# Prompt attention of a hybrid decoder step: both KV groups at once, pipelined by one item

## The chip, the core and the metric

The kernel runs on one core of a Trainium2 chip. The metric is the device time of one execution in microseconds (us); less is better. Engines are named as in the profile: PE (TensorE, matmuls; PEld is its weight load), DVE (VectorE), ACT (ScalarE), POOL (GpSimd) and SP (SyncE, which issues DMAs). Each engine works through its own queue in order, and engines wait for one another by semaphores.

## What is computed

One step of one decoder layer: a half feed-forward block, a mixer, a second half feed-forward block and a final norm, for a prompt of 512 tokens and for 8 sampled sequences of one token with 2048 past tokens. The mixer runs a short convolution beside an attention with three branches: compressed keys, selected blocks of keys, and a window. There are 8 heads in 2 KV groups of 4, each of 64 columns. For the prompt, as 512 tokens have no more blocks than the selection takes and no more tokens than the window, selected and window branches are both plain causal attention, each on its own keys and values. Cut to what matters:

```python
def nsa_core(q, t, kc, vc, kb, vb, kw, vw, kw_pos, gates):
    s = jnp.einsum('btghd,bngd->btghn', q, kc).astype(jnp.float32) * scale
    p_cmp = jax.nn.softmax(jnp.where(m, s, NEG), axis=-1) * m
    o_cmp = jnp.einsum('btghn,bngd->btghd', p_cmp.astype(vc.dtype), vc)
    ...
    s = jnp.einsum('btghd,btgnkd->btghnk', q, kg).astype(jnp.float32) * scale
    ...
    o_sel = jnp.einsum('btghnk,btgnkd->btghd', p.astype(vg.dtype), vg)
    s = jnp.einsum('btghd,bkgd->btghk', q, kw).astype(jnp.float32) * scale
    ...
    o_win = jnp.einsum('btghk,bkgd->btghd', p.astype(vw.dtype), vw)
    return gates[..., 0:1] * o_cmp + gates[..., 1:2] * o_sel + gates[..., 2:3] * o_win
```

## The kernel before

All data stay in SBUF with features or tokens on the 128 partitions; weights are streamed from HBM. A weight unit is split by ACT into a high part (`hi`, L623) and by POOL into the remainder (`lo`, L534), and `unit` (L1454) multiplies them on PE. This holds for the feed-forward blocks, the mixer's input projection, the merge (units U_M3 and up) and the output projection. Between the input projection and the merge lies the attention; for the sampled tokens first their keys are turned and scored, then the prompt's compressed keys are built, then comes the stage that is changed.

The stage is a loop over j, four head pairs: head j of group 0 on partitions 0 to 63 of `Q[:, j]`, head j of group 1 on partitions 64 to 127. For each j there are six blocks b = 0 to 5: compressed, selected and window branch of group 0, and the same of group 1. To multiply with one group alone, DVE copies that group's half of Q into `qz`, whose other half is zero (`queries`, L1156), so that every score is a full 128-row matmul. Blocks go through these steps:

- scores (PE, L1610): four matmuls of 128 to 512 key columns, query tile q seeing keys up to its own tile, into PSUM banks 0 to 3; compressed scores (31 keys) into bank 7;
- `stage1` (DVE, L1201): adds the causal mask and takes the row maximum in one instruction (L1220) from PSUM to `sm`, then scales the maximum (L1225);
- `exps` (ACT, L824): exponentials in place, with row sums;
- `stage2` (DVE, L1227): reciprocal of the sum times the branch's gate, then four multiplications (L1250) that scale the probabilities;
- `turns` (PE, L1629): ten 128x128 transposes (L1354) into banks 4 and 5 by turns, emptied by ACT (`empty`, L820);
- `values` (PE, L1647): four matmuls of 64 output partitions into bank 6, on the half that belongs to the group; all six blocks of a j add up there, and the result is split by ACT (`oth`) and DVE (`otl`).

PE's order is written out by hand in `attend` (L1677): for each block its turns, then the scores of the block two further on, then its values. Twice in a j a sampled sequence is put in between (`sampled`, L1662): 21 matmuls over 2 MB of rows in `GB`, which POOL gathers by an indirect DMA (L531) into one of two buffers once the pass that used it is done, and over `wt`, loaded by SP. The result is added up by DVE (L1255, L1258). The last j is written apart: it holds the first merge unit U_M3 between blocks 4 and 5, whose weights ACT splits right behind the last sampled pass.

```python
            def attend(j, last):
                for b in range(6):
                    ...
                    turns(b, j)
                    if b < 4:
                        scores(b + 2, j)
                    ...
                    if b == 0:
                        sampled(j, 0)
                    values(b, j)
                    if b == 3:
                        sampled(j, 1)
```

## Time and profile before

| what | value |
|---|---|
| median of 3 runs | 1541.0 us (1540.9 to 1541.74) |
| profiled execution, first to last instruction (span) | 1539.9 us |
| profiled execution's own time | not listed apart; 1.1 us lie between its span and the median |
| PE, PEld busy | 1482.3 us (96%), 1377.8 us (89%) |
| DVE, ACT, POOL busy | 642.2 (42%), 538.7 (35%), 504.8 us (33%) |
| mean granted PE clock | 0.986 |

Busy time is the time in which an engine had an instruction under way; matmuls are pipelined, so a start-to-start distance tells more than a duration. Durations in the texts are in us unless marked ns. A granted clock of 1.00 is 2.4 GHz, 0.50 is 1.2 GHz. In a row, `out<-in` names the tiles, L is the line in the kernel, and what stands in brackets is idle time before the instruction and what ended it.

### The profile page before, as it was taken

Reading aid. Unit: us, or ns where it says so; the run is one execution under the profiler, and the core shown is the slowest. Engines: PE = TensorE matmul, PEld = TensorE weight load, DVE = VectorE, ACT = ScalarE, POOL = GpSimd, SP = SyncE. Lnnn points to the kernel's source line nnn. Section 1 sums busy time; section 2 is a strip of 40 time slices with the busy share of each in tenths; the row PEclk is TensorE's granted clock in tenths of the full one; section 3 lists DMA queues with packets and bytes.
Section 4 is the critical chain, followed back from the end, with each engine's and each line's share of the span. In section 5 each row is a group of like instructions: output and inputs, shape, how many; then the busy total and the mean of one; then the engine's idle time right before and its main releaser. Section 6 shows DMA issues by size and latency. Waiting matters only on the chain.

```text
span 1539.9 us, 27584 instructions
## 1 busy us (share of the span) xinstructions
PE 1482.3 (96%) x11500; PEld 1377.8 (89%) x11500; DVE 642.2 (42%) x996; ACT 538.7 (35%) x808; POOL 504.8 (33%) x222
## 2 busy tenths in 40 slices
PE   4899999999999999999899999999899999999998
PEld 4899999999999999994376666999899999999997
DVE  5777533220234652953045553211584332023353
ACT  5566644311223222213344443432334432122221
POOL 3100644443444333410100001444444445344440
PEclk9999999999999999999979999999999999999999
DMA  6731132331323523227833331333232233222221
GB/s 192 253 131 55 55 110 82 119 100 55 105 87 103 198 83 83 84 110 276 301 124 132 134 136 60 97 89 102 84 109 83 82 126 95 81 82 82 95 69 55
DMA packets 125457, 173.08 MB, mean 112 GB/s; under 512 B 11658, under 2 KB 118850, under 8 KB 122236
## 3 DMA queue, kind: packets, MB, share of 16 engines
q1 hardware_dynamic: 121372, 121.98, 25.3%
q0 software_dynamic: 3456, 50.33, 8.1%
q8 instruction: 40, 0.66, 0.2%
q14 instruction: 13, 0.11, 0.0%
q10 hardware_dynamic: 576, 0.00, 0.0%
HBM read 168.55 MB, written 7.95 MB: 115 GB/s over the span
## 4 chain that ended last, share of the span: by engine, by line
PE 92%; DVE 3%; DMA 2%; ACT 1%; issue 1%; SPq 0%; ACTq 0%; DVEq 0%
PE bank L1468 69%; PE bank L1410 5%; PE bank L1354 5%; PE bank L1658 2%; PE bank L1626 2%; PE bank L1671 2%; PE bank L1570 2%; DMA GB<-cache_sel_kv,idx 1%; PE bank L1598 1%; DMA XC<-cache_cmp_kv,idx 1%; PE bank L1618 1%; PE bank L1654 1%; PE bank L1673 0%; DVE XT1l L922 0%; DVE tmp L990 0%
## 5 line engine op out<-in xcount | busy, mean ns | idle before, releaser
L540 POOL TENSOR_TENSOR wlo<-raw,whi 128x1024 fp32r<-128x1024 f32 (+3 forms) x183 | 460.6, 2518 | 633.5 <-ACT whi L644 633.1
L644 ACT ACTIVATE whi<-raw 128x1024 fp32r<-128x1024 f32 (+3 forms) x183 | 196.5, 1075 | 655.4 <-PE bank L1468 649.2
L1468 PE MATMUL bank<-xh,whi 128*128 128x260 f32 (+1 forms) x2032 | 410.0, 283 | 2.9 <-issue 1.1
L1468 PE MATMUL bank<-xh,wlo 128*128 128x260 f32 (+1 forms) x2032 | 409.4, 283 | 0.0
L1468 PE MATMUL bank<-xl,whi 128*128 128x260 f32 (+1 forms) x2032 | 408.7, 283 | 0.0
L1468 PEld LDWEIGHTS bank<-xh,whi 128*128 128x128 f32 (+1 forms) x2032 | 312.6, 188 | 5.1 <-issue 2.2
L1468 PEld LDWEIGHTS bank<-xh,wlo 128*128 128x128 f32 (+1 forms) x2032 | 312.4, 188 | 0.3
L1468 PEld LDWEIGHTS bank<-xl,whi 128*128 128x128 f32 (+1 forms) x2032 | 311.6, 188 | 0.3
L1010 DVE TENSOR_TENSOR tmp<-bank,rr 128x520 f32<-128x520 f32 x88 | 61.6, 700 | 276.6 <-PE bank L1468 275.9
L1468 PE MATMUL bank<-hl,whi 128*128 128x260 f32 x704 | 141.9, 283 | 0.0
L1468 PE MATMUL bank<-hh,wlo 128*128 128x260 f32 x704 | 141.6, 282 | 0.0
L1468 PE MATMUL bank<-hh,whi 128*128 128x260 f32 x704 | 141.3, 282 | 0.0
L1468 PEld LDWEIGHTS bank<-hh,whi 128*128 128x128 f32 x704 | 108.5, 188 | 0.0
L1468 PEld LDWEIGHTS bank<-hh,wlo 128*128 128x128 f32 x704 | 108.4, 188 | 0.0
L1468 PEld LDWEIGHTS bank<-hl,whi 128*128 128x128 f32 x704 | 108.3, 188 | 0.0
L1017 DVE TENSOR_TENSOR hl<-tmp,hh 128x520 f32 x44 | 90.9, 2066 | 40.2 <-ACT hh L735 40.2
L1024 DVE SCALAR_TENSOR_TENSOR xT<-bank,xT 128x520 f32<-128x520 f32 x32 | 22.4, 700 | 161.1 <-PE bank L1468 161.1
L531 POOL DMA_INDIRECT GB<-cache_sel_kv,idx x16 | 15.1, 942 | 223.1 <-PE bank L1674 129.4
L1354 PE MATMUL bank<-ident,XC 128*128 128x128 f32 x256 | 43.1, 298 | 11.9 <-DMA XC<-cache_cmp_kv,idx 10.7
L961 DVE TENSOR_TENSOR tmp<-tmp,tmp 128x520 f32<-128x520 f32 x21 | 53.5, 2547 | 0.7
L922 DVE TENSOR_TENSOR XT0l<-bank,XT0h 64x512 fp32r<-64x512 f32 x64 | 44.2, 690 | 16.5 <-ACT XT0h L675 15.9
L922 DVE TENSOR_TENSOR XT1l<-bank,XT1h 64x512 fp32r<-64x512 f32 x64 | 44.1, 690 | 15.4 <-ACT XT1h L675 14.1
(273 smaller groups left out, 1881.9 us busy)
## 6 DMA issues: line engine op xcount, KB each, us to landing
raw<-ffn_w_gate SPq DMA_DIRECT2D x22, 1024.0 KB, 5.3
raw<-ffn_w_up SPq DMA_DIRECT2D x22, 1024.0 KB, 5.3
raw<-w_mix_in SPq DMA_DIRECT2D x17, 1024.0 KB, 5.1
raw<-ffn_w_down SPq DMA_DIRECT2D x8, 1536.0 KB, 6.5
raw<-ffn_w_down SPq DMA_DIRECT2D x8, 1280.0 KB, 5.8
wt<-win_kv_sample SPq DMA_DIRECT2D x16, 512.0 KB, 3.9
raw<-w_mix_out SPq DMA_DIRECT2D x4, 1024.0 KB, 4.9
win_kv_sample<-state_win_kv SPq DMA_DIRECT2D x1, 4088.0 KB
```

What stands on the lines that cost most here:

```text
L540: pool.tensor_tensor(tile(wlo, w, k, u), raw_tile(u), tile(whi, w, k, u).bitcast(F32), ALU.subtract)\
L644: act.activation(dst, src, ACT.Copy).then_inc(hi_done, 1)
L922: ins = tt(dst, src, hi_.bitcast(F32), ALU.subtract)
L961: ins = tt(ssq[:, :], ssq[:, :], tmp[6][:, :], ALU.add)
L1010: tt(two(dst[:, :]), acc(g), two(rr[:, :]), ALU.mult).then_inc(acc_free, 1)
L1017: tt(hl[:, c, :].rearrange("p o t -> p (o t)"), tmp[1 + j][:, :], hh[:, c, :].rearrange("p o t -> p (o t)").bitcast(F32), ALU.subtract).th ...
L1354: return pe.transpose(dst, src, ident[0:n, 0:n])
L1410: ins = pe.matmul(hid, w[:, kk, j, :], x[kk][b % 2][:, s, r:r + NCMP, :].rearrange("p c g -> p (c g)"), start=(s + r + n == 0), stop=(s == ...
L1468: ins = pe.matmul(acc(g)[0:m, h, :], w[:, u % WS, c, 0:m], x[:, c, h * HT:(h + 1) * HT], start=(c == 0 and n == 0), stop=(c == k - 1 and n ...
L1570: pe.matmul(bank[0:64, q % 5, :], qps[q // 5][:, :], kt[q % 2][:, :], start=False, stop=False, skip_group_check=True).then_inc(kt_used, 1)
L1626: pe.matmul(bank[:, q, 0:(q + 1) * P], qz[:, g, q * P:(q + 1) * P], k[:, 0:(q + 1) * P], start=True, stop=True)\
L1658: ins = pe.matmul(out[:, k * P:SEQ], rows[:, k, c:c + HD], ptp[:, k, k * P:SEQ], start=False, stop=(b % 3 == 2 and k == 0))
```

## The change

The loop now runs over eight items n; item n is head pair j = n // 2 and the selected (n even) or window branch (n odd), for both groups at once. `qz` and its copies are gone: scores take 64 rows of `Q` and of the keys, group 0 on rows 0 to 63 and group 1 on rows 64 to 127, into two banks, with the groups alternating; the four banks hold two query tiles at a time, so the later four of eight scores wait until DVE has read the earlier ones. Values alternate between the groups' two halves of the output partitions, 128 columns at a time. The compressed branch is done once a j for both groups, with the keys of both side by side. Transposes go into chunks of four, four and two tiles, whose evictions alternate between ACT and DVE. The scaling of the probabilities moves from DVE to POOL, which has the gathers for the sampled pass in the same queue. The order is one of a pipeline: the scores of n + 1 come ahead of the turns of n. All loops of the stage are written out. The core of the diff:

```diff
+        ITEMS = 2 * HPG
+
+        def chunk_no(n, g, c):
+
+
+            first = n // 2 * 13 + n % 2 * 7
+            return first + (3 if g == 2 else c if g == 0 else (4 if n % 2 == 0 else 3) + c)
+
+        def chunk_size(c):
+            return (4, 4, 2)[c]
 
         def load_pages(eng, first):
...
-                    else:
-                        pool.wait_ge(sv_done, b - 1)
-                    gather(GB[b % 2], 1, b, gb_loaded[b % 2])
+            for b in range(DB):
+                if b == 0:
+                    pool.wait_ge(lo_done, U_M3)
+                elif b == 1:
+                    pool.wait_ge(grp_done, group(U_M3 - 2) + 1)
+                else:
+                    pool.wait_ge(tp_done, TB + 5 * (b - 1))
+                gather(GB[b % 2], 1, b, gb_loaded[b % 2])
+            for b in range(2):
+                pool.wait_ge(tp_done, TB + 5 * (DB - 1 + b))
+                gather(GB[b % 2], 1, b, gb_loaded[b % 2])
+            for n in range(ITEMS):
+                for g in range(KVH):
+                    pool.wait_ge(fct_ready, 2 * n + g + 1)
+                    for q in range(QT):
+                        v = sm[n % 2][g][:, q * (q + 1) // 2 * P:(q + 1) * (q + 2) // 2 * P]
+                        pool.tensor_scalar(v, v, fct[:, n % 2, q, g:g + 1], None, ALU.mult).then_inc(big_p, 1)
+                if n + 2 < DB:
+                    pool.wait_ge(sv_done, n + 1)
+                    gather(GB[n % 2], 1, n + 2, gb_loaded[n % 2])
...
+            exps(0, 0)
+            for n in range(ITEMS):
+                j = n // 2
+                exps(n, 1)
+                if n % 2 == 0:
+                    cmp_exps(j)
+                    if j:
+                        out_hi(j - 1)
+                empty(n, 0)
+                if n + 1 < ITEMS:
+                    exps(n + 1, 0)
+                else:
+                    act.wait_ge(sv_done, DB)
+                    hi(U_M3)
+                if n % 2 == 0:
+                    empty_cmp(j)
+                empty(n, 1)
+            hi(U_M3 + 1)
+            out_hi(HPG - 1)
 
             for u in range(2, 4):
...
+            def big_max(n, qs):
+
+                if qs[0] == 0 and n >= 2:
+                    dve.wait_ge(pt_tp, chunk_no(n - 2, 1, 2) + 1)
+                for q in qs:
+                    for g in range(KVH):
+                        dve.wait_ge(big_s, 8 * n + 2 * q + g + 1)
+                        dve.memset(bump[:, 4 + 2 * q + g:5 + 2 * q + g], 0.0)
+                        dve.tensor_tensor_reduce(sm[n % 2][g][:, q * (q + 1) // 2 * P:(q + 1) * (q + 2) // 2 * P],
+                                                 bank[:, 2 * (q % 2) + g, 0:(q + 1) * P], tri[:, SEQ - (q + 1) * P:SEQ], 1.0, -3e38,
+                                                 ALU.add, ALU.max, nmx[:, n % 2, q, g:g + 1])\
+                            .then_inc(big_rd, 1)
+
+            def big_neg(n):
+
+                dve.wait_ge(big_rd, 8 * n + 8)
+                ts(nmx[:, n % 2, :, :], nmx[:, n % 2, :, :], -SCALE, None, ALU.mult).then_inc(big_nm, 1)
+
+            def factors(n, g):
+
+                dve.wait_ge(big_exp, 8 * n + 4 * g + 4)
+                pp.did(dve.reciprocal(fct[:, n % 2, :, g], lsm[:, n % 2, :, g]))
+                pp.wait()
+                tt(fct[:, n % 2, :, g], fct[:, n % 2, :, g], gates(n // 2, 1 + n % 2)[:, :, g], ALU.mult).then_inc(fct_ready, 1)
...
+            for n in range(ITEMS):
+                j = n // 2
+                if n + 1 < ITEMS:
+                    big_max(n + 1, range(3))
+                    factors(n, 0)
+                    big_max(n + 1, range(3, QT))
+                    big_neg(n + 1)
                 else:
-                    dve.wait_ge(vn_done, 1)
-                    pp.wait()
-                    pp.did(ts(om[:, :], bank[0:64, 7, 3 * P:4 * P], sst[:, 15:16], None, ALU.mult))
-                    pp.wait()
-                    omg = om[:, :].rearrange("p (g d) -> p g d", g=KVH)
-                    pp.did(tt(omg, omg, gmask[:, :].unsqueeze(2).to_broadcast([64, KVH, HD]), ALU.mult))
-                    pp.wait()
-                    tt(o64[:, :], o64[:, :], om[:, :], ALU.add).then_inc(o64_ready, 1)
-                dve.wait_ge(o_hi, j + 1)
-                tt(otl[:, bass.ds(j, 1), 0:SEQ].rearrange("p o t -> p (o t)"), bank[:, 6, :],
-                   oth[:, bass.ds(j, 1), 0:SEQ].rearrange("p o t -> p (o t)").bitcast(F32), ALU.subtract).then_inc(o_lo, 1)
-                if not last:
-                    pp.end(HPG - 1)
-
-            dve.memset(bump[:, 0:1], 0.0).then_inc(sv_rd, 1)
-            stage1(0, 0)
-            stage2(0, 0)
-            stage1(1, 0)
-            with dve.Fori(0, HPG - 1) as j:
-                attend(j, False)
-            attend(HPG - 1, True)
+                    factors(n, 0)
+                factors(n, 1)
+                if n % 2 == 0:
+                    cmp_norm(j)
+                if n % 2 == 0 and j:
+                    out_lo(j - 1)
+                empty(n, 0)
+                sampled(n)
+                if n % 2 == 0:
+                    empty_cmp(j)
+                empty(n, 1)
+                if n % 2 and j + 1 < HPG:
+                    cmp_max(j + 1)
...
+            def scores(n):
+
+
                 for q in range(QT):
-                    pe.wait_ge(big_p, j * 16 + (4 * n + q + 1))
-                    pe.wait_ge(tp_ev, j * 18 + (TBP + t + q - 1))
+                    for g in range(KVH):
+                        r = slice(HD * g, HD * (g + 1))
+                        i = 8 * n + 2 * q + g
+                        if i >= 4:
+                            pe.wait_ge(big_rd, i - 3)
+                        pe.matmul(bank[:, 2 * (q % 2) + g, 0:(q + 1) * P], Q[r, n // 2, q * P:(q + 1) * P],
+                                  kv[r, 4 + n % 2, 0:(q + 1) * P], start=True, stop=True).then_inc(big_s, 1)
...
+            def turns(n, g):
+
+                for c in range(3):
+                    t = chunk_no(n, g, c)
+                    bank_free(t)
+                    for m in range(4 * c, 4 * c + chunk_size(c)):
+                        q = (0, 1, 1, 2, 2, 2, 3, 3, 3, 3)[m]
+                        pe.wait_ge(big_p, 8 * n + 4 * g + q + 1)
+                        ins = turn(bank[:, 4 + t % 2, (m - 4 * c) * P:(m - 4 * c + 1) * P], sm[n % 2][g][:, m * P:(m + 1) * P])
+                    ins.then_inc(pt_tp, 1)
...
+            def values(n):
+
+
+                t = chunk_no(n, 1, 2)
+                for t in (t - 1, t):
+                    pe.wait_ge((pt_act, pt_dve)[t % 2], t // 2 + 1)
+                for q in range(QT):
                     for k in range(q + 1):
+                        for g in range(KVH):
+                            c = (1 + n % 2) * ROW + P + g * HD
+                            ins = pe.matmul(bank[HD * g:HD * (g + 1), 6, q * P:(q + 1) * P], rows[:, k, c:c + HD],
+                                            prob(g, q * (q + 1) // 2 + k), start=False, stop=(n % 2 == 1 and k == QT - 1))
                 ins.then_inc(pv_done, 1)
...
+            for n in range(ITEMS):
+                j = n // 2
+                if n + 1 < ITEMS:
+                    scores(n + 1)
+                else:
+                    sampled(n)
+                turns(n, 0)
+                if n + 1 < ITEMS:
+                    sampled(n)
+                else:
+                    pe.wait_ge(big_rd, 8 * ITEMS)
+                    unit(U_M3, xh, xl)
+                if n % 2 == 0:
+                    turns_cmp(j)
+                turns(n, 1)
+                if n % 2 and j + 1 < HPG:
+                    cmp_scores(j + 1)
+                if n + 1 == ITEMS:
+                    pe.wait_ge(sv_rd, 1 + DB)
+                    pe.matmul(bank[0:64, 7, 3 * P:4 * P], e8[:, :], srows[:, ROW + P:2 * ROW], start=True, stop=True)\
+                        .then_inc(vn_done, 1)
+                if n % 2 == 0:
+                    values_cmp(j)
+                values(n)
```

## Rows read from the trace of the kernel before

**Rows 1.** Busy time by stretches: stretch, length, each engine's busy time, PE clock, DMA.

```profile
797.51:836.26 38.75, 38.11 (x216) 25.16 (x216) 19.04 (x84) 17.08 (x53) 1.88 (x2) 1.00 0.36 136
...
913.79:958.11 44.32, 41.12 (x251) 29.02 (x251) 18.69 (x69) 18.91 (x54) 4.97 (x2) 1.00 0.19 60
```

**Rows 2.** Timeline of PE inside pairs 1 and 2: start us, busy us, line, operands, count.

```profile
855.49 0.62 PE L1354 MATMUL bank<-ident,cm 128*31 128x128 f32 x4
855.95 2.32 PE L1626 MATMUL bank<-kv,qz 128*128 128x128 f32 x8
858.21 1.07 PE L1654 MATMUL bank<-ptc,vcP 31*64 31x512 f32 x2
859.21 3.71 PE L1671 MATMUL bank<-GB,pst 128*64 128x128 f32 x32
...
863.94 1.68 PE L1354 MATMUL bank<-ident,sm 128*128 128x128 f32 x10
865.66 1.07 PE L1618 MATMUL bank<-kcP,qz 128*128 128x31 f32 x8
866.66 2.37 PE L1658 MATMUL bank<-ptp,rows 128*64 128x128 f32 x8
868.96 1.68 PE L1354 MATMUL bank<-ident,sm 128*128 128x128 f32 x10
870.47 2.32 PE L1626 MATMUL bank<-kv,qz 128*128 128x128 f32 x8
```

**Rows 3.** Line L1383 from 51.0 to 51.5 us: count, duration ns min/median/max, starts us.

```profile
L1383 PE MATMUL bank<-SH,w x4: 272/298/323, 51.0 to 51.2; 128*64 128x127 f32 x4
```

**Rows 4.** Busy time by stretches, columns as in rows 1, where the clock changed.

```profile
755.65:759.14 3.49, 0.00 (x1) 0.00 (x1) 0.00 (x0) 0.00 (x0) 0.21 (x1) 1.00 0.98 397
760.37:763.78 3.41, 3.41 (x7) 1.00 (x6) 0.00 (x0) 0.73 (x2) 0.00 (x0) 0.50 1.02 432
774.03:794.50 20.47, 19.98 (x88) 18.14 (x88) 7.50 (x21) 8.18 (x15) 0.00 (x0) 0.50 0.38 137
```

**Rows 5.** Timelines of PE and of DVE at the first scores of all.

```profile
790.88 4.19 PE L1626 MATMUL bank<-kv,qz 128*128 128x128 f32 x8
...
795.21 0.06 DVE L1218 MEMSET bump<- 128x1 f32 x1 [1.79 <-PE bank L1626]
```

**Rows 6.** Timeline of DVE through maxima, factors and scaling of one item.

```profile
839.67 0.29 DVE L1220 CUSTOM_DVE_ANT_0 sm<-bank,tri 128x128 f32<-128x128 f32 x1
...
839.89 0.42 DVE L1220 CUSTOM_DVE_ANT_0 sm<-bank,tri 128x256 f32<-128x256 f32 x1
...
840.24 0.55 DVE L1220 CUSTOM_DVE_ANT_0 sm<-bank,tri 128x384 f32<-128x384 f32 x1
...
840.72 0.69 DVE L1220 CUSTOM_DVE_ANT_0 sm<-bank,tri 128x512 f32<-128x512 f32 x1
...
841.54 0.18 DVE L1244 RECIPROCAL fct<-lsm 128x4 f32<-128x4 f32 x1
...
842.08 1.27 DVE L1250 TENSOR_SCALAR sm<-sm,fct 128x128 f32<-128x128 f32 x4
```

**Rows 7.** POOL by form, 940 to 1000 us: count, busy us, mean ns, idle before, releaser.

```profile
L540 POOL TENSOR_TENSOR wlo<-raw,whi 128x1024 fp32r<-128x1024 f32 x8 | 20.1, 2509 | 57.8 <-ACT whi L644 57.8
L540 POOL TENSOR_TENSOR wlo<-raw,whi 128x512 fp32r<-128x512 f32 x5 | 6.5, 1290 | 8.2 <-ACT whi L644 8.2
```

**Rows 8.** Tile GB: time from the issue of a gather to its landing.

```profile
DMA to landing us min/median/max: 8.5/8.9/12.2
```

**Rows 9.** ACT's and POOL's timelines and the chain in time order, at unit U_M3.

```profile
941.84 1.06 ACT L644 ACTIVATE whi<-raw 128x1024 fp32r<-128x1024 f32 x1 [1.34 <-PE bank L1674]
...
942.98 2.36 POOL L540 TENSOR_TENSOR wlo<-raw,whi 128x1024 fp32r<-128x1024 f32 x1 [39.00 <-ACT whi L644]
...
947.58 5.97 PE bank L1468 x48
```

More of the change, by code:

```diff
@@ L837, in attend @@
-            def attend(j, last):
-                for b in range(1, 5):
-                    exps(b + 1, j)
-                    if last and b == 4:
-                        act.wait_ge(sv_done, DB)
-                        hi(U_M3)
-                    empty(b, j)
-                if last:
-                    hi(U_M3 + 1)
-                empty(5, j)
-                if not last:
-                    exps(0, j, 1)
-                    exps(1, j, 1)
-                act.wait_ge(pv_done, j * 6 + 6)
-                act.activation(oth[:, bass.ds(j, 1), 0:SEQ].rearrange("p o t -> p (o t)"), bank[:, 6, :], ACT.Copy)\
-                    .then_inc(o_hi, 1)
-                if not last:
-                    empty(0, j, 1)
@@ new lines, in _ @@
+            dve.wait_ge(cpo_done, 2)
+            pp.did(dve.memset(cm[0][:], 0.0))
+            pp.wait()
+            cmp_max(0)
+            big_max(0, range(QT))
+            big_neg(0)
+            for n in range(ITEMS):
[5 more added lines that the diff above has]
+                    big_neg(n + 1)
+                else:
+                    factors(n, 0)
[11 more added lines that the diff above has]
+                    cmp_max(j + 1)
@@ L1647, in values @@
-            def values(b, j):
-                g, t = b // 3, [1, 5, 9, 10, 14, 18][b]
-                pe.wait_ge(tp_ev, j * 18 + (TBP + t))
-                out = bank[HD * g:HD * (g + 1), 6, :]
-                if b % 3 == 0:
-                    if g == 0:
-                        pe.wait_ge(o_lo, j + 1)
-                    pe.matmul(out, vcP[:, g * HD:(g + 1) * HD], ptc[:, :], start=True, stop=False).then_inc(pv_done, 1)
-                    return
-                for k in reversed(range(QT)):
-                    c = (b % 3) * ROW + P + g * HD
-                    ins = pe.matmul(out[:, k * P:SEQ], rows[:, k, c:c + HD], ptp[:, k, k * P:SEQ], start=False,
-                                    stop=(b % 3 == 2 and k == 0))
-                ins.then_inc(pv_done, 1)
@@ L1673, in sampled @@
                     pe.matmul(out, pst[:, 16 + t, :], wt[s][:, t, P:2 * P], start=False, stop=False)
-                pe.matmul(out, pst[0:NCMP, 20, :], vcS[:, bass.ds(j * 2 + s, 1), :].rearrange("p o e -> p (o e)"),
-                          start=False, stop=True).then_inc(sv_done, 1)
-            def attend(j, last):
-                for b in range(6):
-                    if last and b == 5:
-                        pe.wait_ge(big_rd, 16 * HPG)
-                        unit(U_M3, xh, xl)
-                    turns(b, j)
-                    if b < 4:
-                        scores(b + 2, j)
-                    elif not last:
-                        if b == 4:
-                            pe.wait_ge(qz_ready, j + 2)
-                        scores(b - 4, j, 1)
-                    if b == 0:
-                        sampled(j, 0)
-                    values(b, j)
-                    if b == 3:
-                        sampled(j, 1)
-                    if b == 4 and last:
-                        pe.wait_ge(sv_rd, 1 + DB)
-                        pe.matmul(bank[0:64, 7, 3 * P:4 * P], e8[:, :], srows[:, ROW + P:2 * ROW], start=True, stop=True)\
-                            .then_inc(vn_done, 1)
-            pe.wait_ge(qz_ready, 1)
+                pe.matmul(out, pst[0:NCMP, 20, :], vcS[:, b, :], start=False, stop=True).then_inc(sv_done, 1)
             pe.wait_ge(cpo_ev, 2)
-            scores(0, 0)
+            cmp_scores(0)
             pe.wait_ge(keys_rd, 1)
-            scores(1, 0)
+            scores(0)
             pe.wait_ge(ps_ready, 1)
```

317 lines of the change are left out of this document (144 added, 173 removed).

## The prediction

> **What bounds the kernel now.** The busy shares of the whole span (table above) say TensorE (PE), 96%, but an average says nothing of this stage. So the first view is the table by stretches, cut at the first probability turn of each head pair j, from which the reader is to see who is idle here. The four pairs run from 797.51 to 958.11 us: 38.75 us for a plain one, 44.32 for the last, which also holds the first merge unit [rows 1]. In the plain one PE is busy for 38.11 us, DVE for 19.04, ACT for 17.08, POOL for 1.88 at full clock: the stage is PE's own work, and only what shortens or idles PE counts. Then the timeline of PE, which prices a pass by the start of one group to the start of the next [rows 2]; one pair holds two of each compressed group and sampled pass and four of the others: compressed turns 0.46, scores of one group and branch 2.26, compressed values 1.00, sampled values 4.73 (859.21 to 863.94), compressed scores 1.00, values 2.30, turns of ten tiles 1.51. One pair is 4 x (1.51 + 2.26 + 2.30) + 2 x (0.46 + 1.00 + 1.00) + 2 x 4.73 = 38.7, as measured.
>
> **Scores, values, compressed branch: what goes.** Values now write two column halves in turn. That halves of columns run together is in the trace: L1383's four 127-column instructions, on two column halves, start within 51.0 to 51.2 us [rows 3]; on one and the same half an instruction of 128 columns takes 0.11 (the sampled pass, 42 in 4.73 [rows 2]), and four starts would spread over 0.33. So values of both groups cost 2.30 an item, not 4.60. For scores on two row halves no row shows a pair. Bounds: 2.26 an item (as columns do) and 4.52 (one after the other); I take 2.26, by the nearest row. The Trainium skill's page "TensorEngine Tiling (Array Packing)", Key Properties, says that different tiles load weights and multiply in parallel; by it the sum is the one taken here, and rows 3 agree for columns only. The compressed branch goes from two of each per pair to one: 2.46 less. PE's own work is then 2.26 + 2 x 1.51 + 4.73 + 2.30 + 1.00 = 13.3 for an odd item and 13.8 (0.46 and 1.00 in place of one 1.00) for an even one, 27.1 a pair.
>
> **What the new order makes PE wait for.** An item issues scores(n+1) and then turns(n, group 0), with sampled(n) behind these, so all waits stand in PE's queue and everything behind waits too. From the start of scores(n+1):
> 1. Four of the eight scores wait for banks that DVE must have read, and DVE works out no factor for item n until it has done the maxima of q = 0 to 2. First scores are seen at about 0.55, an estimate: the second of two instructions starts some 0.1 to 0.15 in, takes 0.27 to 0.32 [rows 3], and DVE began 0.14 after the group that ended at 795.07 [rows 5]. Maxima start 0.22, 0.35 and 0.48 apart [rows 6]; each now has its own memset of 0.06 [rows 5]; two groups: 2 x 1.23 = 2.46. DVE is through at 3.0.
> 2. Reciprocal and gate factor: 0.54 (841.54 to 842.08 [rows 6]). With a hop POOL starts at 3.6.
> 3. POOL multiplies 128 + 256 + 384 + 512 columns, four instructions, in place of DVE. No row shows POOL doing this. Bounds: DVE's four took 1.27 [rows 6]; POOL's own two-input subtraction takes 1.29 for 512 and 2.51 for 1024 columns [rows 7], 2.38 ns a column and 0.07 an instruction, so 3.3. Same operation on one side, same engine on the other: I take the middle, S = 2.3. The Trainium skill's page "GPSIMD Engine Reference", Engine selection, says that one-input work runs at about line rate and two-input work about twice as slow as on VectorE; by it S is near 1.3 and the sum 7 us lower. Rows 7 agree for two inputs, none shows one.
> 4. PE may turn the last four tiles when q = 3 is scaled: 4 x 0.15 = 0.6 and a hop of 0.1. PE leaves turns(n, 0) at 3.6 + 2.3 + 0.7 = 6.6 instead of 2.26 + 1.51 = 3.8. **2.8 us of every item become a wait.**
> Behind it an odd item has sampled 4.73, turns 1.51, compressed scores 1.00, values 2.30: 16.1. Evictions there fit beside the compressed scores. An even item has 0.46 and 1.00 in place of 1.00 and some 0.1 of eviction: 16.6; where DVE, not ACT, evicts the compressed chunk (j even), it first adds up the sampled result, two operations and their waits, 0.5 by estimate: 17.1.
>
> **Covers.** ACT (17.08 of 38.75 [rows 1]) hands half of its evictions to DVE and has over 12 us for each group's exponentials. DVE loses four scalings of 1.27 a pair and gains evictions; factors of group 1, the compressed normalisation, the low half of the output and an eviction must end before sampled(n) does, at 11.3; with POOL done at 3.6 + 2 x 2.3 = 8.2 that is so by over 1 us. POOL's gather for n+2 now stands behind two scalings and the wait for sampled(n), and scaling of n+1 behind it: 0.94 of issue (two in 1.88 [rows 1]) against some 8 us until it is wanted. Its data land 8.9 us after issue, 12.2 at most [rows 8], with over 25 us until sampled(n+2). SP's loads keep their triggers; no DMA is added. If an item shrank below some 10 us, these covers would be gone.
>
> **Start and end.** Scores(0), at half clock, took 4.19 (clock 0.50 up to 794.50 [rows 4, 5]); eight half-row scores move as many columns, but the last wait for DVE, now behind them instead of beside: the loop starts 0.5 later, at 798.0. Item 7 has no scores ahead: sampled 4.73, turns 1.51. Then unit U_M3 needs its weights, and ACT splits these only after its last eviction of that group: eviction and hops 0.7 (estimate), ACT 1.06, POOL 2.36 [rows 9], so PE stands for 4.1; before, this lay beside turns and values. After an idle 3.49 us the clock was at 0.50 for a stretch of 3.41 us [rows 4]; I charge 2.0 for such a fall here (half of that stretch is 1.7). Unit 5.97 [rows 9], turns 1.5, the new key's matmul 0.4 (as the compressed turns), values 2.3 after 0.5 of waiting (estimate), weights of the next unit 0.8 late (ACT and POOL again, from the last ACT eviction, against the rest of the turns and the values): 23.8.
>
> **The sum.** 798.0 + 17.1 (n = 0) + 3 x 16.1 (odd) + 2 x 16.6 (n = 2, 6) + 17.1 (n = 4) + 23.8 = 937.5, against 958.1: 20.6 us less. What follows is unchanged. The span of 1539.9 becomes 1519.3; the profiled execution lies 1.1 under the median of the runs (1541.0), so I add that: **1520**.
>
> **Rivals.**
> *POOL is the bound (slower).* Each us of S costs 7 us (items 0 to 6). At S = 2.3 + 20.6 / 7 = 5.2 the gain is gone; at S = 6 the time is 1520 + 26 = 1546. Against it: the dearest POOL row gives 3.3. For it: the instruction has never run here and takes its factor from memory. 0.06.
> *The clock falls in the gap between scores and sampled values.* PE would have only transposes and waits there for some 3.6 us of each item. The trace has a fall after 3.49 us without work [rows 4] and none in the pairs, where turns follow matmuls closely. One half-clock stretch of 3.41 in each of seven items costs 7 x 1.7 = 12: 1532; twice that long, 1544. 0.17.
> *Halves don't run together* (the change does not do what it says). Columns: 8 x 2.30 = 18 more, 1538. Rows alone: PE then paces DVE, and step 1 ends 0.65 later: 4.5 more, 1525, inside the forecast. 0.05 for columns.
> *The waits are hidden after all,* PE alone sets the pace: items of 13.3 and 13.8 save 7 x 2.8 and a little more, 1500. It would need DVE's maxima to run beside earlier PE work, which the order of its queue forbids. 0.08.
> The forecast itself, S from 1.27 to 3.3 (-7, +7) and rows alone, is 0.64 and covers 1512 to 1532.
>
> **How the numbers follow.** 0.2% (3 us) is what a measurement of this kernel can tell. Faster by more: the forecast (0.64), the hidden waits (0.08), most of the clock's cases (0.12), some of the columns' (0.02): 0.86. Within: 0.05. Slower: POOL (0.05), the long clock falls (0.03), columns with one of these (0.01): 0.09. The range runs to 1507 below (part of the hidden waits) and to 1537 above (the short clock falls), and leaves out POOL as the bound, serial columns and long falls.
>
> **What would show it.** Right: matmuls of values in pairs some ns apart; per item one idle stretch of PE before its turns, put down to POOL's scaling, and 16 to 17 us from one sampled pass to the next; POOL's scaling between 1.3 and 3.3 for four; PE idle about 4 us before U_M3. Wrong: pairs following each other by their full length; granted clock under 1.0 inside the items; idle time of PE put down to DVE's evictions, or to a gather; a scaling over 5 us.

## The result and the profile after

Measured: **1550.0 us** (median of 4 runs, 1549.4 to 1551.3) against 1541.1 for the kernel before on the same chip (4 runs); the ratio is 1.0056 with an interval of 1.0042 to 1.0071. The change made the kernel slower by some 9 us; 1520 was forecast, and 1550 lies above the range of 1507 to 1537.

The page of the profiled execution (1551.3 us), its busy times and its row of granted clock by fortieths of the span:

```profile
PE 1465.8 (95%) x11636; PEld 1383.8 (89%) x11636; DVE 633.5 (41%) x965; ACT 521.0 (34%) x760; POOL 572.9 (37%) x286
PEclk9999999999999999999968888999999999999999
```

The eights stand where prompt attention is. Next the table by stretches (stretch, length, busy time and count of PE, PEld, DVE, ACT, POOL, granted clock, DMA share, GB/s): items 0 to 6 from the first score of item 1 to the sampled pass of item 7; item 1 alone; item 7; and the first and the last of seven stretches, one in each item:

```profile
799.24:944.85 145.61, 120.58 (x874) 94.60 (x875) 63.28 (x272) 51.46 (x159) 68.01 (x65) 0.84 0.30 116
821.37:841.58 20.21, 16.84 (x128) 13.77 (x126) 8.28 (x37) 6.22 (x20) 9.52 (x9) 0.83 0.29 114
944.85:968.46 23.61, 18.51 (x156) 17.03 (x153) 5.08 (x8) 3.75 (x6) 10.95 (x8) 0.86 0.15 45
...
806.61:813.44 6.83, 5.84 (x28) 5.48 (x28) 1.23 (x3) 3.00 (x10) 5.21 (x5) 0.50 0.01 2
...
929.50:936.30 6.80, 5.56 (x23) 4.43 (x24) 3.10 (x7) 2.77 (x9) 6.22 (x6) 0.50 0.01 4
```

Before, a pair (two items) took 38.75 us at full clock with PE idle for 0.6 [rows 1]. Now item 1 alone takes 20.21: PE idles for 3.4 of it, and the clock is 0.83, since in every item some 6.8 us run at its lower level (1.2 GHz in place of 2.4). Both show in PE's timeline of that item (start, busy, line, operands, count, idle time ahead and what ended it):

```profile
821.37 3.07 PE L1679 MATMUL bank<-kv,Q 64*128 64x128 f32 x16
825.53 0.30 PE L1404 MATMUL bank<-ident,sm1g 128*128 128x128 f32 x1 [1.09 <-POOL sm1g L627]
826.35 0.44 PE L1404 MATMUL bank<-ident,sm1g 128*128 128x128 f32 x2 [0.51 <-POOL sm1g L627]
827.57 0.90 PE L1404 MATMUL bank<-ident,sm1g 128*128 128x128 f32 x3 [0.78 <-POOL sm1g L627]
829.11 1.11 PE L1404 MATMUL bank<-ident,sm1g 128*128 128x128 f32 x4 [0.64 <-POOL sm1g L627]
830.15 5.51 PE L1738 MATMUL bank<-GB,pst 128*64 128x128 f32 x32
835.50 1.04 PE L1740 MATMUL bank<-wt,pst 128*64 128x128 f32 x8
836.38 0.38 PE L1741 MATMUL bank<-vcS,pst 127*64 127x128 f32 x2
836.69 1.09 PE L1404 MATMUL bank<-ident,sm1g 128*128 128x128 f32 x8
...
840.83 0.27 PE L1724 MATMUL bank<-pt,rows 128*64 128x128 f32 x1
840.84 0.27 PE L1724 MATMUL bank<-pt1b,rows 128*64 128x128 f32 x1
```

Four times PE waits for POOL to scale the tiles that it is to turn, 3.0 us in all. Then the sampled pass takes 6.54 (830.15 to 836.69), against 4.73 [rows 2], with the clock at its lower level for rather more than the first half of it; it fell while PE did nothing but turns and waits. The last two rows are values of two column halves, 0.01 apart. PE's longest waits over the whole stage (waited for, us in total, times, longest), and POOL's scalings by shape (busy, mean ns) with their time in item 1:

```profile
PE bank L1404 <- POOL sm0g L627: 13.2, 16, 1.8
PE bank L1404 <- POOL sm1g L627: 8.8, 12, 1.1
PE bank L1518 <- issue: 3.9, 1, 3.9
```
```profile
L627 POOL TENSOR_SCALAR sm1g<-sm1g,fct 128x512 f32<-128x512 f32 x8 | 12.5, 1558 | 0.0
L627 POOL TENSOR_SCALAR sm1g<-sm1g,fct 128x384 f32<-128x384 f32 x8 | 9.9, 1238 | 0.0
L627 POOL TENSOR_SCALAR sm1g<-sm1g,fct 128x256 f32<-128x256 f32 x8 | 7.3, 918 | 0.0
L627 POOL TENSOR_SCALAR sm1g<-sm1g,fct 128x128 f32<-128x128 f32 x8 | 4.8, 601 | 29.9 <-DVE fct L1280 29.9
```
```profile
824.78 8.52 POOL L627 TENSOR_SCALAR sm1g<-sm1g,fct 128x128 f32<-128x128 f32 x8 [7.72 <-DVE fct L1280]
```

28 waits for POOL, four in each of seven items, are 22.0 us. Eight scalings take 8.52, so four (S) take **4.26**: above both ends of the prediction's bounds (1.27 and 3.3). The steps come to 2.49 ns a column (1558 less 601, over 384) and 0.28 us an instruction.

### The profile page after: what moved, and what is told of

Same layout as the page of the kernel before. It is cut to its first block, busy times and chain, and to the rows that moved or that the text cites. A ratio compares the mean times of both kernels' runs of the same rounds, so it can differ in the third digit from the quotient of the medians.

```text
span 1549.5 us, 27548 instructions
## 1 busy us (share of the span) xinstructions
PE 1465.8 (95%) x11636; PEld 1383.8 (89%) x11636; DVE 633.5 (41%) x965; ACT 521.0 (34%) x760; POOL 572.9 (37%) x286
## 4 chain that ended last, share of the span: by engine, by line
PE 88%; DVE 4%; DMA 2%; issue 2%; POOL 2%; ACT 1%; SPq 0%; ACTq 0%; DVEq 0%
PE bank L1518 69%; PE bank L1460 5%; PE bank L1404 5%; PE bank L1738 3%; PE bank L1620 2%; DMA GB<-cache_sel_kv,idx 1%; PE bank L1724 1%; PE bank L1648 1%; POOL sm1g L627 1%; DMA XC<-cache_cmp_kv,idx 1%; POOL sm0g L627 1%; PE bank L1740 0%; DVE XT1l L957 0%; DVE tmp L1025 0%; DVE wpe L974 0%
## 5 line engine op out<-in xcount | busy, mean ns | idle before, releaser
L627 POOL TENSOR_SCALAR sm0g<-sm0g,fct 128x128 f32<-128x128 f32 (+3 forms) x32 | 34.1, 1078 | 53.5 <-DVE fct L1280 53.5
L957 DVE TENSOR_TENSOR XT0l<-bank,XT0h 64x512 fp32r<-64x512 f32 x64 | 44.1, 690 | 15.8 <-ACT XT0h L700 15.1
```

Source lines behind the costliest of these rows:

```text
L627: pool.tensor_scalar(v, v, fct[:, n % 2, q, g:g + 1], None, ALU.mult).then_inc(big_p, 1)
L957: ins = tt(dst, src, hi_.bitcast(F32), ALU.subtract)
```

## The experiments

Chips differ a little (the median of the kernel before was 1541.2, 1542.9, 1543.6 and 1541.9 beside e1 to e4, e5 to e8, e9 to e11 and e12), so kernels measured on different chips are compared by their ratio to it; 0.001 is 1.5 us, and intervals reach 0.0011 to 0.003 to either side. A profile shows one execution, and where that is not a typical one, the text says so. The changed kernel stands at 1.0056. Theory A: PE waits for a chain of maxima, factors and POOL's scaling, and the clock falls for that wait. Against it, B: one thing alone sets the pace (POOL's load, or the order, whichever engine scales); C: nearly all of the loss is the clock. Lengths of items below are read off PE's timeline.

| run | what | median us | ratio (interval) |
|---|---|---|---|
| e1 | factors ahead of the maxima | 1525.6 | 0.9897 (0.9879 to 0.9914) |
| e2 | DVE scales | 1542.1 | 1.0001 (0.9987 to 1.0016) |
| e3 | matmuls in the waits | 1537.4 | 0.9971 (0.9959 to 0.9982) |
| e4 | first merge weights early | 1550.0 | 1.0055 (1.0040 to 1.0070) |
| e5 | e1, evictions early too | 1518.6 | 0.9846 (0.9829 to 0.9862) |
| e6 | e2, evictions early too | 1525.9 | 0.9903 (0.9875 to 0.9931) |
| e7 | POOL's two-input form | 1541.4 | 0.9989 (0.9976 to 1.0003) |
| e8 | e5 and e4 | **1516.7** | 0.9831 (0.9814 to 0.9847) |
| e9 | e3 and e7 | 1534.5 | 0.9941 (0.9924 to 0.9958) |
| e10 | e5, values group by group | 1530.4 | 0.9919 (0.9903 to 0.9936) |
| e11 | sampled pass ahead of the turns | 1521.7 | 0.9855 (0.9826 to 0.9884) |
| e12 | e8, e7 and two moves | 1516.6 | 0.9837 (0.9823 to 0.9850) |

**Factors first (e1).**

```
-                    big_max(n + 1, range(3))
                     factors(n, 0)
+                    big_max(n + 1, range(3))
```

> DVE works out the factors of item n, group 0 ahead of the three pairs of maxima of item n+1, instead of behind them; nothing else moves. Theory A (PE waits for a chain, maxima 2.3 us, factors 0.4, POOL's scaling 4.26, in front of the turns, and the clock falls because of that wait): the maxima leave the chain, POOL starts some 2.5 us earlier in an item, the sampled pass starts about 6.0 after the scores instead of 8.8, seven items give 7 x 2.7 = 19 us back: 1531 if the clock still falls in each item, and 1518 if the falls go too (sampled pass 4.73 again instead of 6.5, 7 x 1.8 = 12.6 more). Theory B (POOL's scaling alone sets the pace, whatever is ahead of it, because both groups' 8.5 us and a gather fill POOL's queue): under 1 us an item, 1543 to 1550. Theory C (the clock fall is nearly all of the loss, the waits themselves are covered elsewhere): the wait shrinks but the clock stays at 0.50 for part of each item, 1540 to 1548.

The ratio fell by 0.0159, 24.5 us, between theory A's two numbers: one line moved on DVE gives back more than the change lost. B (POOL sets the pace) and C fall; POOL does the same work in the same 4.26, but out of the path. PE's waits for POOL are gone from the list. Two waits for DVE are new in it (the line left out between them is the merge unit's, 5.0 in two). Why DVE comes late in one of the four is in its own timeline:

```profile
PE bank L1404 <- DVE pt L1291: 9.0, 4, 3.2
...
PE bank L1679 <- DVE nmx L1265: 3.3, 1, 3.3
```
```profile
838.90 0.40 DVE L1249 TENSOR_REDUCE cfc<-cm 128x8 f32<-128x248 f32 x1
...
839.78 0.62 DVE L1255 TENSOR_TENSOR cm<-cm,cfc 128x248 f32<-128x248 f32 x1
840.32 0.68 DVE L1314 TENSOR_TENSOR otl<-bank,oth 128x512 fp32r<-128x512 f32 x1
840.92 0.67 DVE L1291 COPY pt<-bank 128x512 f32<-128x512 f32 x1
```

The eviction of the first turned tiles stands behind the compressed normalisation and the output's low half; PE's third group of turns waits for its bank.

**DVE scales (e2), and again with its evictions early (e6).**

POOL's own scaling goes; this stands behind DVE's factors:

```
+                dve.wait_ge(fct_ready, 2 * n + g + 1)
+                for q in range(QT):
+                    v = sm[n % 2][g][:, q * (q + 1) // 2 * P:(q + 1) * (q + 2) // 2 * P]
+                    ts(v, v, fct[:, n % 2, q, g:g + 1], None, ALU.mult).then_inc(big_p, 1)
e6 as well:
+                empty(n, 0)
                 factors(n, 1)
...
-                empty(n, 0)
```

> The four scalings of each group go back from POOL to DVE, behind the factors of the same group; POOL only gathers. The order of maxima and factors is as in the changed kernel. Theory A: S falls from 4.26 to DVE's 1.27 for four, so the chain is 3.0 shorter in each of seven items, 21 us: 1529 with the clock falls, 1516 without them. Theory B (the order, maxima ahead of factors, is the loss and the engine is not): DVE now has 2.5 us more of work in each item ahead of the maxima's successors, and the time stays within 1540 to 1552. Theory C (clock alone): the idle time shrinks, the falls stay, 1535 to 1545.

> DVE scales instead of POOL, as in the second experiment, maxima still ahead of the factors, but DVE's evictions of group 0 stand ahead of group 1's factors and scaling, of the compressed normalisation and of the output's low half. Tells what the engine alone was worth once no eviction is late. Theory A: the second experiment's 16.4 us in four waits for DVE's evictions go, and its falls at 823.9, 844.4, 899.0 and 919.5: 1542 - 16 - 4 to 7 = 1519 to 1522, near the 1520 forecast with S of 1.3 to 2.3. Rival (DVE itself is the bound when it scales too): 1530 to 1545.

e2 missed: 8.5 us less in place of 21 to 34, and 1542.1 lies inside the ranges of B and C, so e2 alone doesn't tell A from them. Its four scalings do take 1.27 (the first row), but DVE's queue grew and the same eviction came late (the second), with 6.83 us at half clock in each of four items:

```profile
820.17 1.27 DVE L1279 TENSOR_SCALAR sm1g<-sm1g,fct 128x128 f32<-128x128 f32 x4
```
```profile
PE bank L1403 <- DVE pt L1290: 16.4, 4, 5.0
```

With the evictions moved ahead (e6) another 15 us went, to 0.9903, and the clock holds in all seven items: four us above what was expected, with 6.4 us of that wait left in four places, and below the rival's 1530 to 1545. Beside e5, where slow POOL scales behind factors that come early, the engine swap is the lesser cure by some 9 us (4 by the profiled executions, 1518.7 and 1522.7, where e6's median is 1525.9): in these runs the place in the order weighs more than how long the operation takes. No run has DVE scale behind factors that come first, so what the engine is worth in that order stays open.

**Matmuls in the waits (e3).**

```
                     for m in range(4 * c, 4 * c + chunk_size(c)):
+                        if g == 0 and n + 1 < ITEMS and m in (0, 1, 3, 6):
+                            for _ in range({0: 4, 1: 2, 3: 3, 6: 2}[m]):
+                                pe.matmul(bank[:, 7, 3 * P:4 * P], ident[:, :], ident[:, :], start=True, stop=True)
```

> Adds 11 matmuls of 128 columns (identity by identity, into a bank part that nobody reads) between the turns of group 0 in items 0 to 6, where PE otherwise waits for POOL's scaling; the waits themselves stay, and the output is not touched. 77 matmuls of 0.055 to 0.11 us, about 1 us an item, lie inside a wait of 2 to 4 us. Theory A (waits and clock falls both cost, the falls 1.8 us an item): the granted clock stays at 1.00 through the items, the sampled pass is 4.73 again, and the time is 1550 - 12 = 1538. Theory C (the clock is most of the loss): 1530 or less. Theory B, or a clock that doesn't follow PE's gap: the falls stay, 1549 to 1554.

13.1 us less by the ratios, 12 expected by A. PE does more work and still waits on POOL's pace, and the clock holds; the stretch from 1.3 us ahead of item 0's first score (800.47) to the end of item 6:

```profile
799.20:930.96 131.76, 121.40 (x1037) 98.21 (x1036) 63.40 (x275) 52.56 (x162) 67.89 (x65) 1.00 0.34 129
```

So the lower clock is a loss of its own, it follows from PE having only turns and waits there, and it is about as large as what the waits cost beyond the forecast (13.1 here, 14.8 in the table below).

**POOL's two-input form (e7), and with matmuls in the waits (e9).**

```
-  pool.tensor_scalar(v, v, fct[:, n % 2, q, g:g + 1], None, ALU.mult).then_inc(big_p, 1)
+  pool.tensor_tensor(v, v, fct[:, n % 2, q, g:g + 1].to_broadcast([P, (q + 1) * P]), ALU.mult).then_inc(big_p, 1)
```

> The changed kernel, with POOL's scaling as a multiplication of two tensors (the factor broadcast along the row) in place of one tensor by a scalar from memory; nothing else moves. Prices the form. If POOL pays 2.38 ns a column and 0.07 an instruction here, as its subtraction does: S is 3.3 instead of 4.26, each of seven items 0.96 shorter, 1550 - 7 = 1543, the falls as before. Rival (a broadcast operand or this size costs as much as the scalar form): S 4.2 to 4.4, 1549 to 1551.

> The third and the seventh together: POOL scales by the two-input form (S = 2.9 as that run showed), and 8 matmuls whose result nobody reads stand in PE's wait of items 0 to 6, to keep the clock. Asks whether the forecast was right but for S and for the clock; by its own price of 7 us for each us of S, S = 2.9 gives 1520 + 4 = 1524. Theory A: 1537.4 (third) - 1.36 x 7 = 1528, with no half-clock stretch in the items. Rival (a cover is gone as well: in the seventh, PE waited 5.9 us for DVE's evictions, a wait that the changed kernel hides behind POOL's): 1531 to 1535.

The form is cheaper than either theory had it:

```profile
L627 POOL TENSOR_TENSOR sm1g<-sm1g,fct 128x512 f32<-128x512 f32 x8 | 8.3, 1037 | 0.0
...
L627 POOL TENSOR_TENSOR sm1g<-sm1g,fct 128x128 f32<-128x128 f32 x8 | 3.2, 398 | 35.1 <-DVE fct L1280 34.7
```

With 824 and 610 between, S is 2.87 for group 1 and 2.96 for group 0. 1.36 us of S at 7 us each would be 9.5, and e7 is 10.3 us below the changed kernel. That the two agree is luck: the time at half clock in the items fell as well, from 47.8 us (7 x 6.83) to 23.9, and 5.9 us of waits for DVE's eviction came in. At this S the clock holds in items 1, 4 and 5 (16.81, 17.19, 16.81 us), falls for 3.41 in items 0 and 3 (19.48 and 18.07) and for 10.24 and 6.83 in items 2 and 6, where DVE's eviction is late as well; items 1 and 2:

```profile
818.71:835.52 16.81, 14.43 (x129) 11.45 (x127) 8.88 (x37) 6.22 (x20) 6.48 (x9) 1.00 0.37 131
835.52:858.65 23.13, 18.64 (x126) 14.14 (x124) 10.66 (x40) 6.72 (x20) 6.64 (x9) 0.78 0.34 132
```

e9 came out in the rival's range (1531 to 1535): the fill and the cheaper form add up only in part, since this wait for DVE (6.2 us in four) takes over. Items 2 and 6, where it is longest, took 22.9 and 21.8, the others 16.56 to 17.85. Against theory A the clock still falls in those two, for 6.83 and 3.41 us; item 2:

```profile
832.17:855.03 22.86, 19.41 (x143) 15.55 (x141) 10.67 (x40) 6.73 (x20) 6.66 (x9) 0.85 0.33 130
```

**First merge weights early (e4).**

```
                 if n + 1 < ITEMS:
...
-                else:
-                    act.wait_ge(sv_done, DB)
-                    hi(U_M3)
+                if n + 1 == ITEMS:
+                    act.wait_ge(sv_done, DB)
+                    hi(U_M3)
                 empty(n, 0)
```

> ACT splits the first merge unit's weights ahead of its evictions of the last item's group 0 instead of behind them; nothing else moves. Theory A (in the last item PE stands 3.9 us for these weights, as one term of the loss apart from the items): the wait of 3.9 goes to under 1 and the half-clock stretch at 953 with it, 4 to 6 us less: 1544 to 1546. Rival (the sampled values' last result is what the split waits for, or POOL's subtraction of 2.4 us comes late whatever ACT does): the wait stays above 3, 1549 to 1551.

In its profile PE's wait ahead of the unit is 1.7 in place of 3.9, but the ratio did not move (1.0055). Where 1.7 are left, POOL's subtraction of these weights starts only when group 1 is scaled (946.99), so ACT was about half of the cause. The profiled execution took 1545.95, e4's other four 1549.9 to 1550.4, and in two of the profiled items the clock falls for 3.41 in place of 6.83, so it is not typical. Why the medians don't show the 2 us stays open; whatever the unit's wait is worth, it is no large part of the loss.

**Evictions early too (e5), and all three (e8).**

```
                 factors(n, 1)
+                empty(n, 0)
                 if n % 2 == 0:
                     cmp_norm(j)
...
-                empty(n, 0)
```

> Factors of group 0 ahead of the maxima, as in the first experiment, and DVE's evictions of group 0's turned tiles ahead of the compressed normalisation and the output's low half. Theory A (PE's loss is what stands ahead in other engines' queues; in the first experiment 9.0 us in four waits had moved to DVE's eviction, behind those two): the four waits go, and with them the half-clock stretches at 841.7 and 906.5; 1525.6 - 9.0 - 2 to 4 = 1513 to 1515, and PE's items are 13.3 to 14.5. Rival (POOL's 8.5 us of scaling an item now sets the pace, or the normalisation becomes late in its place): the waits come back under another name, 1521 to 1527.

> As the fifth (factors first, evictions of group 0 ahead), and ACT splits the first merge unit's weights ahead of its evictions of the last item's group 0. The version meant to beat both kernels. Theory A: 1 to 4 us less than the fifth, 1510 to 1513, with PE's wait ahead of that unit at 1.7 instead of 3.9. Rival (the same as the fifth, since the clock falls there all the same): 1513 to 1515.

e5 gave 8 us more than e1 and stays 4 above A's range: the wait for DVE's eviction fell from 9.0 only to 5.0 (row below), and PE's 3.3 us in item 0 stay (there the factors, now first, need the first exponentials), with 6.83 us at half clock in that item. The two falls that were to go are gone, and items 1 to 6 take 14.5 to 16.2 in place of 13.3 to 14.5.

```profile
PE bank L1404 <- DVE pt L1291: 5.0, 4, 1.3
```

e8, at 0.9831, is below e5 by 2 us, with intervals that overlap, and so as far above its own range; its wait ahead of the unit is 1.7 as in e4. It beats both kernels: 26 us less than the one before. An odd and an even item of e8:

```profile
819.60:834.99 15.39, 13.73 (x128) 11.46 (x126) 7.75 (x37) 6.22 (x20) 7.64 (x8) 1.00 0.39 153
834.99:851.15 16.16, 14.65 (x126) 11.19 (x124) 8.64 (x40) 6.73 (x20) 11.48 (x12) 1.00 0.46 180
```

PE is idle for 1.7 and 1.5 of them.

**Values group by group (e10).**

```
-                for q in range(QT):
-                    for k in range(q + 1):
-                        for g in range(KVH):
+                for g in range(KVH):
+                    for q in range(QT):
+                        for k in range(q + 1):
```

> The fifth kernel with the values of group 0 all ahead of those of group 1, instead of one of each in turn; sums and instructions are the same. Prices the claim that two column halves run together, where PE sets the pace. If they do: one item's values take 2 x 1.1 to 2 x 2.3 instead of 2.3, up to 2.3 more in eight items, 1518.5 + 18 = 1536 (PE does each instruction of 128 columns in 0.11). Rival (the pairs gain nothing): 1518 to 1520.

11 us more than e5, at the same sums and counts: the column halves do run together. It is less than 18 because an item's values took 4.1 us, not 4.6 (from the first row to the second, the next item's scores):

```profile
830.41 2.07 PE L1724 MATMUL bank<-pt,rows 128*64 128x128 f32 x17
...
834.54 0.71 PE L1679 MATMUL bank<-kv,Q 64*128 64x128 f32 x6
```

8 x (4.1 - 2.3) = 14, as items 1 to 5 are each 1.8 longer. By the two profiles all eight items together are 13.3 longer; e10's stage began 3.4 us earlier than e5's, which hides part of it in the spans.

**Sampled pass ahead of the turns (e11), and a last trim (e12).**

```
e11, PE:
                 if n + 1 < ITEMS:
                     scores(n + 1)
-                else:
-                    sampled(n)
+                sampled(n)
                 turns(n, 0)
...
e12, DVE, the order of item 0's factors left as in the changed kernel:
+                empty(n, 0)
+                if n + 1 < ITEMS:
+                    big_neg(n + 1)
                 factors(n, 1)
```

> Sampled(n) between scores(n+1) and the turns of group 0 on PE (DVE adds its result up ahead of the evictions of group 0), factors of group 0 ahead of the maxima except in item 0, first merge unit's weights early. Theory A (what is left to lose in the eighth, 1516.7, is PE's wait for DVE's evictions and, in item 0, 3.3 us for the factors): items of 14.7 and 15.2 instead of 15.4 and 16.2, 5.6 less, and 3 less at the start: 1507 to 1510. Rival (turns and values without a pass between them put ACT's and DVE's evictions on PE's path, or POOL's scaling of group 1 comes late): 1514 to 1520.

> The eighth kernel with POOL's scaling in the two-input form, DVE's evictions of group 0 also ahead of the negated maxima and of group 1's factors, and in item 0 the first three pairs of maxima ahead of the factors as in the changed kernel (there the factors wait for the first exponentials, and scores(1) for them: 3.3 us in the eighth). Theory A (what the eighth still loses are these waits): 2 to 3 less in item 0, 0.4 less in each of four items: 1512 to 1514.5. Rival (group 1's factors come too late for POOL, or item 0 pays POOL's 2.9 in place of the 3.3): 1516 to 1520.

Both missed. e11's median lies above even its rival's range (1514 to 1520), e12's inside its own rival's (1516 to 1520). In e11 the turns of both groups follow each other, so evictions by ACT (3.5, 2.3 and 1.1) and DVE (2.9) are waited for, as the rival said, and with PE on turns and short waits the clock falls again, for 6.83 us in item 1 and in item 5 and 3.41 in item 2:

```profile
PE bank L1406 <- ACT pt1a L863: 3.5, 3, 1.3
PE bank L1406 <- DVE pt L1291: 2.9, 6, 0.8
```
```profile
816.71:835.32 18.61, 16.77 (x128) 14.14 (x126) 7.84 (x37) 6.22 (x20) 9.78 (x10) 0.83 0.59 223
```

Two of e11's four executions took 1518.4 and 1518.6 us at a mean granted clock of 0.981 and 0.983, two 1524.9 (the profiled one) and 1526.6 at 0.976 and 0.975, so these falls need not be in every execution. Beside e8, whose clock holds in items 1 to 6, the profile suggests that the sampled matmuls between the two groups' turns keep the clock and cover the evictions; as DVE's order moved too, it is no proof. e12's items 1, 2, 5 and 6 are 0.5 shorter than e8's, as A had it (0.4), but item 0 takes 20.5 in place of 20.3 (it waits for POOL again), and group 1's factors, now behind the evictions, make POOL late where it must also split the merge unit's weights; PE starts the unit when that subtraction ends, at 924.39, after 5.2 us of waiting (1.7 in e8; e12's profiled execution took 1520.75, its median is 1516.6):

```profile
919.20 2.80 POOL L627 TENSOR_TENSOR sm1g<-sm1g,fct 128x128 f32<-128x128 f32 x4 [6.50 <-DVE fct L1280]
921.96 2.33 POOL L558 TENSOR_TENSOR wlo<-raw,whi 128x1024 fp32r<-128x1024 f32 x1
```

## Why the prediction was wrong

The seven items, from the first score of one to that of the next (the last to item 7's sampled pass), in us:

| item | 0 | 1 | 2 | 3 | 4 | 5 | 6 | sum |
|---|---|---|---|---|---|---|---|---|
| forecast, S = 2.3 | 17.1 | 16.1 | 16.6 | 16.1 | 17.1 | 16.1 | 16.6 | 115.7 |
| e3: S = 4.26, clock kept | 19.38 | 17.92 | 19.29 | 18.08 | 18.71 | 17.93 | 19.18 | 130.5 |
| the changed kernel | 22.13 | 20.21 | 21.30 | 20.09 | 20.91 | 19.92 | 21.05 | 145.6 |

- **Columns and rows together: right.** Values start in pairs 0.01 apart, and one item's take 2.3; e10 prices it. Scores of both groups take 3.07 for 16 instructions, DVE's maxima setting the pace as forecast; one group after the other would have taken 4.52, the prediction's upper bound, so rows run together as well. The Trainium skill's page "TensorEngine Tiling (Array Packing)", Key Properties, says that tiles work in parallel; the runs agree, for columns by e10 and for rows by the 3.07.
- **Steps 1 and 2: right.** From the scores' start at 821.37, DVE was through with the maxima of q = 0 to 2 after 2.9 (forecast 3.0) and POOL began after 3.4 (3.6):

```profile
824.31 0.17 DVE L1278 RECIPROCAL fct<-lsm 128x4 f32<-128x4 f32 x1
824.52 0.17 DVE L1280 TENSOR_TENSOR fct<-fct,gt 128x4 f32<-128x4 f32 x1
```
- **Step 3, POOL's scaling: this failed.** Forecast 2.3, bounds 1.27 to 3.3, measured 4.26. The bound was drawn from the dearest POOL row, a subtraction of two tensors, as if one tensor and a scalar could not cost more. They do. (Its remark that rows 7 agree for two inputs had no VectorE row beside it; in e1's profile above, DVE's subtraction of 512 columns takes 0.68, POOL's 1.29 [rows 7].) By the prediction's own price, 1.96 x 7 = 13.7 us; the e3 row stands 14.8 above the forecast, so the price and the rest of the sum (moves, 9.5 behind the turns) were sound at this S. e9's items 1 and 4 say nearly the same: 16.82 and 17.19 at S = 2.9, where the forecast's 16.1 and 17.1 become 16.7 and 17.7. PE's wait, forecast at 2.8 us an item, is what grew: it left the turns of item 1 at 8.8 (830.15) in place of 6.6.
- **The clock: left out of the sum, and wrongly kept apart.** The rival had the place right (scores, then turns and waits, then a slow sampled pass) but was priced as an alternative at S = 2.3, with 3.41 or twice that at half clock. It was 6.8 in each of seven items, 15.1 us in the table (13.1 by the ratios), less than the 24 that the rival took for twice 3.41, since part of each stretch is spent waiting for POOL. And it came with the long S: in e7, at 2.9, three of seven items keep the clock. So the two rivals were in the main one event. Alone, S = 4.26 gives 1520 + 13.7 = 1534 (e3 measured 1537.4 with the clock kept), still faster than before, and the clock's 15.1 alone about as much; together 1549, against the 1550 that ran.
- **Start, item 7, the rest.** The stage began at 799.24 (798.0 forecast), mostly because work ahead of it ran late in this execution (below). Item 7 took 23.61 (23.8), with PE idle for 3.9 ahead of the unit (4.1). Together 1.2 - 0.2 = 1.0 us. 14.8 + 15.1 + 1.0 is the 31 by which the stage ended late (968.46 in place of 937.5).
- **The break-even was set too high.** The prediction put it at S = 5.2, clock kept, and gave "POOL is the bound" 0.06. With the clock falling it lies much lower, between the 2.9 of e7 (ratio 0.9989, no change) and the 4.26 of the change.
- **A cover that it called sound had a hole.** The prediction let an eviction by DVE end as late as the sampled pass does (11.3). But the last two turns of group 0 need its bank, and they stand ahead of that pass. DVE's evictions of group 0 are in time only while POOL is slower: in item 2 of the changed kernel the eviction ends 8.5 after the first score and the sampled pass starts at 9.2. With PE through the turns at 6.6, as forecast, it would have been late there, by estimate from these two times. As soon as POOL's wait shrinks (e1, e2, e7, e9), it is late behind the normalisation and the output's low half, 6 to 16 us in four places. It cost next to nothing in the changed kernel itself.

## What to carry to other kernels

Before moving work to an idle engine, look where its result stands in the path of the busiest one: here the same slow scaling is waited for nowhere once its factors are worked out ahead of the maxima (e1, e5), and moving it back to the fast engine without that helped less (e2, e6). Price an operation that no row shows with room above the dearest row of that engine, not with that row as the top. And when a wait is added between turns on PE, charge the lower clock in the same case as the wait: here the longer wait brought it, and other matmuls in the wait kept it away (e3).

## What the runs showed of the hardware

- **On POOL, tensor by scalar from memory was slower than tensor by broadcast tensor.** The same multiplication of 512 columns took 1558 ns as tensor by scalar, 1037 to 1123 as tensor by broadcast tensor. The steps from 128 to 512 columns are 2.49 ns a column against 1.66 to 1.89, and POOL's subtraction has 2.38 [rows 7]. The Trainium skill's page "GPSIMD Engine Reference", Engine selection, calls one-input work on that engine roughly line-rate, and dearer only with two inputs; for this form the measurement says otherwise and decides.
- **Some of DVE's short operations are held up beside POOL.** Means of the factor's multiplication (four columns, two inputs), first in the changed kernel, then in e6, where POOL scales nothing:

```profile
L1280 DVE TENSOR_TENSOR fct<-fct,gt 128x4 f32<-128x4 f32 x16 | 4.7, 294 | 0.7
```
```profile
L1275 DVE TENSOR_TENSOR fct<-fct,gt 128x4 f32<-128x4 f32 x16 | 2.7, 166 | 0.5
```

The first mean mixes two cases. Eight of the sixteen end before POOL starts and take 0.17 (824.52 above); the other eight run beside its scaling, and six of them take 0.49:

```profile
826.38 0.49 DVE L1280 TENSOR_TENSOR fct<-fct,gt 128x4 f32<-128x4 f32 x1
```

The same page of the Trainium skill, Specifications, says that POOL shares its memory interfaces with VectorE and contends with its two-input instructions; these rows agree in direction. But two-input operations are not always held up: the compressed factor's (128x8) took 0.74 in the changed kernel, 0.48 in e7 and 0.17 in e8, each time beside a running scaling, and what decides it is not shown. In the changed kernel it is off PE's path. In e7 it is not: in item 2, what DVE does from the negated maxima to the late eviction takes 4.2 us, against 2.4 in e1.
- **The same code may lose clock in one execution and not in another.** In unchanged work ahead of the stage, the changed kernel's profiled run had 3.4 us at half clock, and that of the kernel before, at the same place, had none:

```profile
700.80:704.20 3.40, 3.40 (x8) 1.01 (x6) 3.33 (x3) 0.60 (x1) 0.00 (x0) 0.50 0.89 283
```
```profile
701.80:705.20 3.40, 3.40 (x14) 1.22 (x12) 3.33 (x3) 1.07 (x3) 0.00 (x0) 1.00 0.92 282
```

PE had 8 instructions under way in it in place of 14. Six of the thirteen profiles of the changed kernel and its variants (the changed kernel, e2, e3, e7, e10, e12) have this fall, and seven don't, with the same code ahead of the stage. Their first scores start between 789.3 and 793.3 us, so single profiles differ by up to 4 us before the stage begins, and stages are better compared by their own lengths than by the span.
